# Two-layer retention/pooling trunk on one core: six of the twelve transposed chunks of h move from TensorE to DMA transposes

## What is computed

```python
for i in range(DEPTH):              # 0: retention, 1: causal pooling
    h = h + mixer_i(rms_norm(h, norm_i))           # output product into h
    gate = jax.nn.sigmoid(rms_norm(h, ple_norm[i]) @ ple_w_gate[i])
    h = h + gate * (p[i] @ ple_w_proj[i])
return rms_norm(h, final_norm)
```

## Time and profile before

| | |
|---|---|
| median of 3 runs | 1567.12 us (1567.09 to 1567.23) |
| the profiled execution | 1566.8 us, span 1565.0 us |
| PE busy | 1550.7 us of the span, 99% |
| DVE, ACT busy | 1018.5 us, 844.6 us |
| granted TensorE clock | 0.998 of full speed |
| DMA | 314.71 MB, mean 201 GB/s |

### The profile page before, as it was taken

One profiled execution on the slowest core, in us unless ns is written; L12 is line 12 of the kernel. 1 busy time (PEld: TensorE's weight loads), 2 busy tenths in 40 slices (PEclk: granted clock), 3 DMA queues, 4 the chain that ended last, 5 costly groups with the idle time before them and its releaser, 6 DMA issues.

```text
span 1565.0 us, 19252 instructions
## 1 busy us (share of the span) xinstructions
PE 1550.7 (99%) x6938; PEld 1283.0 (82%) x6938; DVE 1018.5 (65%) x1247; ACT 844.6 (54%) x1000; POOL 4.6 (0%) x12
## 2 busy tenths in 40 slices
PE   9999999999999999999999999999999999999997
PEld 6888888888888888888888888888888888888885
DVE  5766666666666666667656485675577557755665
ACT  6454554635555464555645556644664476445553
POOL 0000000000000000000000000000000000000000
PEclk9999999999999999999999999999999999999999
DMA  9565555747556554755455666755665566554451
GB/s 374 220 227 190 188 201 198 204 165 237 188 176 212 197 198 182 227 183 193 160 192 191 189 225 213 216 203 190 223 212 206 194 208 223 213 207 169 181 193 76
DMA packets 102581, 314.71 MB, mean 201 GB/s; under 512 B 63968, under 2 KB 63984, under 8 KB 66960
## 3 DMA queue, kind: packets, MB, share of 16 engines
q1 hardware_dynamic: 42272, 295.45, 52.8%
q10 hardware_dynamic: 59568, 15.48, 5.1%
q0 software_dynamic: 704, 3.27, 0.5%
HBM read 297.40 MB, written 2.10 MB: 191 GB/s over the span
## 4 chain that ended last, share of the span: by engine, by line
PE 97%; ACT 1%; DVE 1%; DMA 0%; ACTq 0%; issue 0%; SPq 0%; DVEq 0%
PE accA L354 12%; PE accA L355 12%; PE accA L356 12%; PE accC L354 11%; PE accC L356 11%; PE accC L355 11%; PE accB L354 8%; PE accB L355 8%; PE accB L356 8%; PE side L370 1%; DMA w_raw<-in_stream_dram 0%; PE side L408 0%; PE side L407 0%; PE side L409 0%; ACTq L672 0%; ACT w_hi L615 0%
## 5 line engine op out<-in xcount | busy, mean ns | idle before, releaser
L956 DVE TENSOR_TENSOR w_lo<-w_raw,w_hi 128x1024 fp32r<-128x1024 f32 x551 | 666.7, 1222 | 410.1 <-ACT w_hi L615 408.2
L615 ACT CAST w_hi<-w_raw 128x1024 fp32r<-128x1024 f32 x551 | 574.5, 1053 | 545.8 <-PE accB L356 181.2
L354 PE MATMUL accC<-w_hi,xa_hi 128*128 128x512 f32 x512 | 199.4, 389 | 0.7 <-DVE w_lo L956 0.7
L355 PE MATMUL accC<-w_lo,xa_hi 128*128 128x512 f32 x512 | 199.2, 389 | 0.0
L356 PE MATMUL accC<-w_hi,xa_lo 128*128 128x512 f32 x512 | 199.2, 389 | 0.0
L354 PE MATMUL accA<-w_hi,xa_hi 128*128 128x512 f32 x508 | 197.8, 389 | 0.8 <-DVE w_lo L956 0.8
L356 PE MATMUL accA<-w_hi,xa_lo 128*128 128x512 f32 x508 | 197.6, 389 | 0.0
L355 PE MATMUL accA<-w_lo,xa_hi 128*128 128x512 f32 x508 | 197.6, 389 | 0.0
L354 PEld LDWEIGHTS accC<-w_hi,xa_hi 128*128 128x128 f32 x512 | 96.1, 188 | 21.0 <-DVE w_lo L956 1.1
L354 PEld LDWEIGHTS accA<-w_hi,xa_hi 128*128 128x128 f32 x508 | 95.4, 188 | 21.0 <-DVE w_lo L956 1.3
L356 PEld LDWEIGHTS accC<-w_hi,xa_lo 128*128 128x128 f32 x512 | 96.1, 188 | 20.0
(11 more groups left out here) (209 smaller groups left out, 2183.2 us busy)
## 6 DMA issues: line engine op xcount, KB each, us to landing
w_raw<-in_stream_dram SPq DMA_DIRECT2D x275, 1024.0 KB, 4.8
h<-in_x_dram SPq DMA_DIRECT2D x4, 512.0 KB, 13.7
xT_raw<-in_xT_dram SPq DMA_DIRECT2D x3, 512.0 KB, 15.4
dec<-in_decay_dram POOLq DMA_DIRECT2D x1, 1024.0 KB, 9.5
fgain<-in_final_gain_dram POOLq DMA_DIRECT2D x1, 1024.0 KB, 6.4
out_dram<-emb SPq DMA_DIRECT2D x1, 1024.0 KB, 3.8
halvesT<-halves ACTq DMA_TRANSPOSE x56, 3.7
w_raw<-in_stream_dram SPq DMA_DIRECT2D x2, 256.0 KB, 6.3
```

What stands on the lines that cost most here:

```text
L354: pe.matmul(acc[pair][t][:, 0:n], xh, wh, start=first and b == 0, stop=False)
L355: pe.matmul(acc[pair][t][:, 0:n], xh, wl, start=False, stop=False)
L615: act.copy(w_hi[:, r % RING, :], w_raw[:, r // 2, (r % 2) * 1024:(r % 2 + 1) * 1024]).then_inc(hi_ready, 1)
L956: dve.tensor_tensor(w_lo[:, r % RING, :], w_raw[:, r // 2, (r % 2) * 1024:(r % 2 + 1) * 1024], w_hi[:, r % RING, :].bitcast(F32), ALU.subt ...
```

## The change

Chunks (1,0), (2,0), (2,1), (2,2), (3,0) and (3,1) are no longer transposed by PE. ACT makes their halves (`h_halves`), issues two DMA transposes with the next unit, and eight units after the halves joins the words and makes the hi part (`h_words`); DVE makes the lo part from `words`. The first gate product of a layer reads its k-tiles in the order of `ORDER`, with the weight stream laid out to match, so that chunk (1,0) is used last in layer 0 and (3,1) last in layer 1.

```diff
+POOL_TURNS = TURNS + NC
+LATE = 3
+CLOSE_TURNS = POOL_TURNS + 4 * GROUPS - 2
+ORDER = ((1, 2, 3, 0), (0, 2, 3, 1))
+HT = [(1, 1), (1, 2), (1, 3), (2, 3), (3, 2), (3, 3)]
+Z0 = EMB_U + NC * RO_U
+H_TURNS = (((1, 0, EMB_U + RO_U + 2, EMB_U + RO_U + 10),) + tuple((2, c, Z0 + KD_U * (c + 1) + 3, Z0 + KD_U * (c + 1) + 11) for c in range(NC - 1)),
+           ((3, 0, EMB_U + PO_U + 2, EMB_U + PO_U + 10), (3, 1, EMB_U + PO_U + 10, EMB_U + PO_U + 18)))
...
             def h_transposes(stage, c):
 
                 pe.wait_ge(h_ready, NC * (stage - 1) + c + 1)
-                if stage + c > 1:
-                    pe.wait_ge(xT_ready, NC * (stage - 1) + c)
+                if stage != 2 and c > ORDER[stage // 2][1 if stage == 3 else 0]:
+                    pe.wait_ge(xT_ready, NC * (stage - 1) + ORDER[stage // 2].index(c))
+                if stage == 2:
+                    pe.wait_ge(xT_ready, NC)
...
-                        unit(u, base, "ACBC"[z], xb_hi, xb_lo, kz * UNIT, kz == 0, kz == KD_U - 1, seg)
+                        kk = ORDER[layer][kz // 2] * 2 + kz % 2 if z == 0 else kz
+                        unit(u, base, "ACBC"[z], xb_hi, xb_lo, kk * UNIT, kz == 0, kz == KD_U - 1, seg)
                     for cc in range(NC):
-                        if u == EMB_U + ou * (cc + 1):
+                        if u == EMB_U + ou * (cc + 1) and (2 * layer + 1, cc) in HT:
                             h_transposes(2 * layer + 1, cc)
-                        if cc < NC - 1 and layer == 0 and u == EMB_U + NC * ou + KD_U * (cc + 1) + 1:
-                            h_transposes(2, cc)
...
+            def h_halves(stage, c):
+                act.wait_ge(h_ready, NC * (stage - 1) + c + 1)
+                halves_of(h[:, :, c * COL:(c + 1) * COL], in_close[stage // 3])
+
+            def h_words(stage, c, turn):
+                bufs = in_close[stage // 3]
+                if stage == 2 and c:
+                    act.wait_ge(xT_ready, NC * (stage - 1) + c)
+                words_of(turn, bufs, bufs[2])
+                act.wait_ge(words_ready, turn * 2 + 2)
+                stream_hi(stage, c)
...
+                    if first and u == LATE:
+                        h_words(2, NC - 2, POOL_TURNS - 1)
                     if first and u == 4:
                         stream_hi(2, NC - 1)
...
                 for u in range(EMB_U + NC * ou + GATE_U):
+                    for i, (_stage, _c, at_u, _words_u) in enumerate(H_TURNS[layer]):
+                        if u == at_u + 1:
+                            act.wait_ge(halves_ready, (turn0 + i) * 2 + 2)
                     split_hi(u, base, seg, landed(base))
+                    for i, (_stage, _c, at_u, _words_u) in enumerate(H_TURNS[layer]):
+                        if u == at_u + 1:
+                            transpose_halves(in_close[layer])
...
-                        if u == z + 4 and layer == 0:
-                            stream_hi(2, c)
+                    for i, (stage, c, at_u, words_u) in enumerate(H_TURNS[layer]):
+                        if u == words_u:
+                            h_words(stage, c, turn0 + i)
+                        if u == at_u:
+                            h_halves(stage, c)
...
+                    if first and u == LATE:
+                        stream_lo(2, NC - 2)
+                        dve.wait_ge(xT_ready, 2 * NC - 1)
+                        for b in sums:
+                            own.mark(dve.memset(b[:, :, 0:PAD], 0.0))
                     if first and u == 4:
                         stream_lo(2, NC - 1)
                         row_scale(2)
```

More of the change, by code:

```diff
@@ L132, in trunk @@
         xa_lo = sb("xa_lo", [P, KD, SEQ], F32R)
+        oT0 = nc.sbuf_base
         oT_hi = sb("oT_hi", [P, KG, SEQ], F32R)
@@ L137, in trunk, with turn_buffers @@
         emb = sb("emb", [P, TT, D], F32)
-        halves = nc.alloc_sbuf_tensor_at("halves", [P, TT, 2, COL], U16, offset=emb0)
-        halvesT = nc.alloc_sbuf_tensor_at("halvesT", [P, 2 * COL // P, SEQ], U16, offset=emb0 + 4096)
-        words = nc.alloc_sbuf_tensor_at("words", [P, COL // P, SEQ], F32, offset=emb0 + 8192)
+        def turn_buffers(name, a, b, c):
+            return (nc.alloc_sbuf_tensor_at("halves" + name, [P, TT, 2, COL], U16, offset=a),
+                    nc.alloc_sbuf_tensor_at("halvesT" + name, [P, 2 * COL // P, SEQ], U16, offset=b),
+                    nc.alloc_sbuf_tensor_at("words" + name, [P, COL // P, SEQ], F32, offset=c))
+        in_emb = turn_buffers("_e", emb0, emb0 + 4096, emb0 + 8192)
+        words = in_emb[2]
         pT_hi = sb("pT_hi", [P, 2, KP, SEQ], F32R)
         pT_lo = sb("pT_lo", [P, 2, KP, SEQ], F32R)
+        sig0 = nc.sbuf_base
         sig = sb("sig", [P, TT, COL], F32)
@@ L188, in trunk @@
         fgain = at("fgain", 32, [P, D], F32)
+        half_oT = KG // 2 * SEQ * 4
+        in_close = (turn_buffers("_r", oT0 + half_oT, oT0 + KG * SEQ * 4 + half_oT, arena0 + 32 * 1024),
+                    turn_buffers("_p", arena0 + 40 * 1024, arena0 + 44 * 1024, sig0))
         acc = {n: [ctx.enter_context(nc.psum_tensor(f"acc{n}{t}", [P, COL], F32)) for t in range(TT)] for n in "ABC"}
@@ L633, in stream_hi @@
                 hi = xb_hi if stage % 2 else xa_hi
-                act.wait_ge(hT_done, NC * (stage - 1) + c + 1)
+                if (stage, c) in HT:
+                    act.wait_ge(hT_done, HT.index((stage, c)) + 1)
                 for j in range(4):
                     k = 4 * c + j
-                    cp = act.activation(hi[:, k, :], side[j // 2][:, (j % 2) * SEQ:(j % 2 + 1) * SEQ], ACT.Copy,
-                                        scale=gain[:, stage, k:k + 1])
+                    src = side[j // 2][:, (j % 2) * SEQ:(j % 2 + 1) * SEQ]
+                    if (stage, c) not in HT:
+                        src = in_close[stage // 3][2][:, j, :]
+                    cp = act.activation(hi[:, k, :], src, ACT.Copy, scale=gain[:, stage, k:k + 1])
                     if j % 2:
@@ L661, in pr_hi_part, with halves_of, transpose_halves, words_of @@
                 act.copy(pr_hi[:], pr[:]).then_inc(pr_hi_ready, 1)
-            def halves_of(src):
+            def halves_of(src, bufs):
                 for t in range(TT):
-                    act.copy(halves[:, t, :, :], src[:, t, :].bitcast(U16).rearrange("p (n two) -> p two n", two=2)
+                    act.copy(bufs[0][:, t, :, :], src[:, t, :].bitcast(U16).rearrange("p (n two) -> p two n", two=2)
                              ).then_inc(halves_ready, 1)
-            def transpose_halves():
+            def transpose_halves(bufs):
                 for t in range(TT):
-                    act.dma_start_transpose(halvesT[:, :, t * P:(t + 1) * P],
-                                            halves[:, t, :, :].rearrange("p two n -> p (two n)")).then_inc(halvesT_landed, 16)
-            def words_of(n, dst):
+                    act.dma_start_transpose(bufs[1][:, :, t * P:(t + 1) * P],
+                                            bufs[0][:, t, :, :].rearrange("p two n -> p (two n)")).then_inc(halvesT_landed, 16)
+            def words_of(n, bufs, dst):
                 act.wait_ge(halvesT_landed, n * (16 * TT) + 16 * TT)
@@ L679, in words_of @@
                     act.copy(dst[:].bitcast(U16).rearrange("p k (n two) -> p two k n", two=2)[:, i, :, :],
-                             halvesT[:, 4 * i:4 * i + 4, :]).then_inc(words_ready, 1)
+                             bufs[1][:, 4 * i:4 * i + 4, :]).then_inc(words_ready, 1)
+            def h_halves(stage, c):
[8 more added lines that the diff above has]
+                stream_hi(stage, c)
             def qk_halves(hd):
                 act.wait_ge(qk_ready, hd + 1)
-                halves_of(qk)
+                halves_of(qk, in_emb)
             def qk_words(hd):
                 act.wait_ge(yT_ready, hd)
-                words_of(hd * 2 - 1, words)
+                words_of(hd * 2 - 1, in_emb, words)
                 act.wait_ge(words_ready, hd * 4)
@@ L694, in y_halves @@
                 act.wait_ge(y_gated, hd + 1)
-                halves_of(yn)
+                halves_of(yn, in_emb)
             def y_words(hd):
                 act.wait_ge(qkT_ready, hd + 1)
-                words_of(hd * 2, words)
+                words_of(hd * 2, in_emb, words)
                 act.wait_ge(words_ready, hd * 4 + 2)
@@ L760, in m_words @@
                     act.wait_ge(mT_ready, n)
-                words_of(turn, words)
+                words_of(turn, in_emb, words)
                 act.wait_ge(words_ready, turn * 2 + 2)
@@ L829, in group @@
                 n2 = g * 2
-                turn = TURNS if first else TURNS - 2 + g * 4
+                turn = POOL_TURNS if first else POOL_TURNS - 2 + g * 4
                 turns = U_FIRST if first else U_LATER
@@ L872, in close @@
                 seg = base % (2 * RAW)
+                turn0 = (TURNS, CLOSE_TURNS)[layer]
                 for u in range(EMB_U + NC * ou + GATE_U):
```

(32 more changed lines are left out.)

12 lines of the change are left out of this document (5 added, 7 removed).

## The result

The changed kernel takes 1587.39 us (median of 4 runs, 1586.65 to 1587.84) against 1567.16 us of the kernel before on the same chip: a ratio of 1.0129, 95% interval 1.0117 to 1.0141, 20.2 us slower. The forecast was 1581.0 us, its range ended at 1586.0. The profiled execution took 1586.99 us with a span of 1585.0, 20.0 more than before.

The account below looks back on a forecast made before the run. PE, in flight 1550.7 of 1565.0 us, was taken as the bound, with ACT's order making it wait. A 5.3 us saving against 19.2 us of added waits gave +13.9, 1581.0 us; forecast 1577.5 to 1583.5, range 1575.0 to 1586.0.

Parts of the forecast that it names:

- (1,0) and (2,0): Layer 0, output products and product z = 1: PE waits before tr(1,1) and at unit 25, +1.0 and +2.6 us.
- z = 2: Layer 0 product taking chunk (2,1): PE waits for w_lo at unit 32, +3.3 us.
- z = 3: Layer 0 product taking chunk (2,2): the same wait at its fifth unit, +3.3 us.
- first pooling group: After z = 3, PE waits at units 4 and 5 behind chunk (2,2)'s words and hi, +4.0 us in all.
- all behind it, with layer 1: Layer 1: savings mostly eaten by late squares and tr(3,3) waiting; between -1.8 and +0.5, taken as -0.3 us.
- the saving on PE: Six chunks' transposes leave PE at 0.88 us each: -5.3 us, the whole gain.
- the argument of the ring: Between a sigmoid and the next product's fifth unit ACT has 10.9 us; in z = 2 and 3 it needs 14.73.
- the dear pair: (2,0)'s two DMA issues, 0.7 us behind SP's load: ACT free 5.57 us after that load, PE late at unit 25.
- the late squares of both layers: Words and hi (4.32 us) among squares at units 16 and 26 delay sigmoids to 773.5 and 1489.05.
- rival 3: Clock falls in two 3.9 us waits, half clock up to 5 us each, +2.5 to +3 twice: 1586.5 us; chance 0.12.
- The rule weighed against the row: Skill's small DMA initiation time gives +9.5 us, 1576.6; rows charging ACT 1.8 us per pair, 4 to 5 dear, give +13.9.
- Rivals 1, 2, 4 and 5: 1: PE never waits, 1561.8 (0.03); 2: only unavoidable waits, 1574.1 (0.10); 4: more dear pairs, 1583-1586 (0.07); 5: same (0.02).

Follow-up runs that it names:

- filler kernel: The changed kernel with extra matmuls on TensorE, their results unread, just ahead of four of its waits; 1580.64 us, ratio 1.0087.
- kernel with early words: The changed kernel with words and hi part of chunks (2,0), (2,1), (2,2) moved three units ahead; 1576.06 us, ratio 1.0057.
- kernel with everything moved: The changed kernel with words of stage 2 three units ahead, halves of (1,0) and (2,c) later, words of (1,0) and (3,1) earlier; 1571.54 us, ratio 1.0027.
- kernel of five chunks: The changed kernel with (2,2) back on TensorE, turns of the other chunks re-placed and stage 3's squares spread; 1564.72 us, ratio 0.9985.
- kernel with the moved pair: The changed kernel with only the two DMA transposes of (2,0) issued at unit 26 instead of unit 24; 1582.58 us.

## Why the prediction was wrong

Measured from boundary to boundary in both traces (the sigmoids, and the first ACT instruction that writes `u`, the pooling layer's first product, as the end of the first pooling group), in the first row less the 0.2 us by which this trace runs late from its start, and in the last column less 1.69 us per lowered stretch:

| place | forecast | whole slip | without the clock |
|---|---|---|---|
| (1,0) and (2,0) | +3.6 | +5.5 | +3.8 |
| z = 2 | +3.3 | +4.8 | +3.1 |
| z = 3 | +3.3 | +4.7 | +3.0 |
| first pooling group | +4.0 | +5.3 | +3.6 |
| all behind it, with layer 1 | -0.3 | -0.4 | -0.4 |
| sum | +13.9 | +19.9 | +13.1 |

- **Right**: the saving on PE, the argument of the ring (14.73 us behind the sigmoid against 10.9), the place of every wait but the 0.50 us at unit 23 (a late sigmoid puts `w_lo` of 23 at 780.9 in the forecast too, but the wait is not in its list), the dear pair, the late squares of both layers. The filler kernel, which keeps all of it but the clock, ran 1580.64 us against the 1581.0 of the forecast, no place of the table is off by more than 0.4 us, and stage 2 alone makes the loss.
- **The step that failed** stands in rival 3: "so 3.9 us should just hold". I took it from the earlier trace rows, full clock for 4.5 us behind PE's last matmul. That row shows when the clock falls behind a kernel's last matmul, once; it does not show what a pause in mid-kernel brings. In the changed kernel the lower clock began 0.8 us after the wait of 2.55 us had ended (790.20), and with the first matmul behind the three others. I gave this case 0.12, and I counted two waits in it; it came behind four, two of them shorter than those I had asked about. Its price was mis-sized too: 1.69 us each, where I had 2.5 to 3, from up to 5 us at half clock, "as long as the wait itself", though the waits I asked about were 3.9 us. Two at 2.5 to 3 gave 1586.5, four at 1.69 gave 1587.4. That rival 3 came within 1 us of the measured time is luck: it had too few falls, each too dear.
- The Trainium skill (TensorE: Matmul & The Clock Gate, Part 1) has an idle PE halve its clock. The traces agree (half speed behind each of the four waits of 2.18 to 3.74 us), and the filler run makes it the cause here; that a wait is dearer than its length, which I cited beside rival 3, came true.
- **The rule weighed against the row.** The Trainium skill (DMA: Bandwidth & Descriptors, Issuing engines are not separate DMA queues) has the time to initiate a DMA usually small beside the DMA itself; the prediction's sum by that rule left the issues out. In layer 0's turns the pairs held ACT for 2.62 us three times and for 5.53 once, so 1.3 us or more for each DMA, and the eight DMAs of these turns (`halvesT_r`) took 2.9 us in the median from issue to landing. Moving one issue by two units was worth 4.8 us. For these DMA transposes the measurement decides against the rule.
- **Rivals 1, 2, 4 and 5** fell. No pair of z = 2 or 3 was dear, and no wait named a DMA.

Open: why waits of 2.2 to 2.9 us end in half speed at one time and not at another. In all traces there were seven such waits: 2.55, 2.27, 2.18 and 2.17 us had a lowered clock behind them, 2.87, 2.46 and 2.33 us had none. All ten of 3.3 us or more had it, none of 1.5 us or less. The DMA share does not separate the three of the kernel with early words (0.83, 0.61 and 0.62, the second with the fall).

## What to carry to other kernels

Price a wait of TensorE by its length and by what follows it: here some 1.7 us, at most 3, had to be added for each wait of 3.3 us or more, and for four of the seven between 2.2 and 2.9 us. Count the waits, and do not go by the longest. A transpose taken off TensorE was paid here on the engine that prepares the operands, so ask at which unit that engine has slack: six chunks cost 20 us in their first places, three of them nothing, and five of them, placed with room, gained 2.4 us. Between issuing a DMA transpose and using it leave as much distance as its slowest landing beside the big loads, and put instructions that are ready ahead of the issue.

## What the runs showed of the hardware

- Of the chunks of h in layer 0, a pair of DMA transposes on ACT took 2.6 us with the last 1 MB load 4.7 us before it (the four of z = 2 and 3 in the changed and the filler kernel), 3.5 to 3.9 us at 1.5 us (three in the kernel with everything moved), 5.3 to 5.5 us at 0.5 us (six in four kernels). The distance does not settle it alone: in the kernel of five chunks one pair took 3.86 us at 3.1 us, the next 2.62 us at 2.4 us.
- ACT's issue of a DMA can run beside casts that stand ahead of it in the program (781.41 against 782.23 and 783.18, in the kernel with the moved pair).
- What is left of the lowered stretch when PE goes on does not grow with the wait ahead of it: 8 matmuls started 0.4 us or more apart behind 3.47 us, 9 behind 14.71, 13 behind 10.14, but 13 behind 3.73 as well, in the kernel with the moved pair.
- The clock can fall after the pause: PE went on at 813.40 in the kernel with early words, and its granted clock was 0.91 from 813 to 815 and 0.50 from 815 to 818.
